# The first norm of a PEER block and its first two query tiles, done in two halves of 256 tokens, with two roundings moved

## The chip, the cores and the metric

The kernel runs on one core of one Trainium2 chip. The metric is the device time of one execution in microseconds (us). Before the change it was 3694.77 us, the median of three runs (3693.27 to 3698.32).

## The reference, cut to what matters

The program computes a two-layer transformer block (adaptive norms, gated feed-forward, token mixing) and then a second block whose last part is a PEER layer. The change touches only the step from the layer norm into that PEER layer. Here `x` has 512 tokens of 1024 channels.

```python
x = layer_norm(DEEPNORM_ALPHA * x + m, ln1_g[l], ln1_b[l])
f = peer_ffn(x, peer_wq[l], peer_keys[l], peer_u[l], peer_v[l])

def peer_ffn(x, wq, sub_keys, u_tab, v_tab):
    q = (xf @ wq).reshape(t, 8, 2, 128)                 # 8 heads, two 128-wide halves each: 16 query tiles
    scores = einsum("thpc,hpnc->thpn", q, sub_keys)     # 128 keys per half
    s_top, i_top = top_k(scores, 16)
    cand = s_top[..., 0, :, None] + s_top[..., 1, None, :]
    best_s, best_pos = top_k(cand, 16)                  # 16 of 16384 experts per token and head
    gates = softmax(best_s)
    # per token and head, over its 16 experts e:
    out += gelu(x . u_tab[e]) * gates[e] * v_tab[e]
```

## The kernel before, in words

Activations stand channels by tokens: `T.xT` is eight tiles k of 128 channels by 512 tokens. Every matrix product with a weight is made of three passes: a weight tile of 128x1024 is loaded by SP's queue into `wraw`, rounded by ACT into `whi` (`round`, line 2114), and POOL makes the remainder `wlo` (`rest`, line 2120); the activations are split in the same way into `xh` and `xl`. A tile's load waits until a buffer's earlier remainder is done (semaphore `w_lo`). The five tiles 8 to 12 (`AHEAD`) go to buffers of their own, but their loads stand in SP's queue behind the load of tile 5, which waits for the remainder of tile 3.

The last stage, `peer` (line 2131), begins when the mean and the reciprocal standard deviation of every token stand ready (`T.mean` in SBUF, `T.psN` in PSUM). The five engines then run lists of instructions that are written out by hand and joined by semaphores:

- Norm. DVE multiplies tile k by `psN` into one of two temporary tiles (line 2585), ACT applies gain and bias (2412) and rounds into `xh` (2416), DVE makes `xl` (2588). The mean is subtracted from tiles 2 to 4 by DVE (2576) and from 5 and 6 by POOL (2212). Each instruction covers all 512 tokens.
- Query tiles 0 and 1. TensorE (PE) takes the eight k in order as they come (`pair`, lines 314 to 318). ACT copies the first 128 tokens' queries (2420), PE scores them against the keys (`first_scores`, 2263), and DVE's `best` and `choose_first` find the 16 experts of the first head for the first 128 tokens.
- A gather (line 2226) is one indirect DMA issued by POOL: 128 tokens' rows of 2048 numbers (1.05 MB), u and v of one expert for each token. There are 512 of them. For the first 96 there are nine slots: five `g_own`, two `g_low` (free once query tile 3 is multiplied), two in `xT` (free once all tokens are transposed into `xtok`, `turn`, 2272). A gather into a used slot waits for the matmul that reads it (`g_mm`).
- Expert work. DVE takes the dot product with u (`dots`, 2532), ACT gelu, gate and a diagonal matrix (`weights`, 2395 to 2407), PE adds diag times v (`experts`, 2311, in the later loop 2348).
- Query tiles 2 to 4 come before the first expert work on PE; each of the tiles 5 to 15 is then cut in two parts, and four sets of two gathers stand between them (`PARTS`). After gather 96 the slots are 16 and only gathers, dots and expert matmuls are left.

POOL's list mixes gathers with the remainders; the rule is

```python
W.rest(pool, 3)
W.rest(pool, 4)
for j in range(OWN):
    gather(j)
W.rest(pool, 5)
for j in range(OWN, EARLY):
    gather(j)
W.rest(pool, 6)
for j in range(EARLY, TOTAL):
    n, at = divmod(j - EARLY + PAIR, ROWS)
    if at == 0 and STEP0 + n + 1 < NQ2 and n > 0:
        W.rest(pool, STEP0 + n + 1)
    gather(j)
```

with OWN 5, EARLY 9, PAIR 2, ROWS 8, STEP0 5, NQ2 16.

Of the kernel before, what the change touches and what calls it, by code (L numbers as in the profile page):

```python
# [15 lines left out]
F32 = mybir.dt.float32  # L16
# [2059 lines left out]


AHEAD = (8, 9, 10, 11, 12)


class Queries(Stream):
# [34 lines left out]
    def rest(self, pool, n):  # L2116
# [3 lines left out]
        self.nc.gpsimd.tensor_tensor(lo, self.raw(n), hi.bitcast(F32), ALU.subtract).then_inc(self.M["w_lo"], 1)  # L2120

    def part(self, pe, n, out, xh, xl, k0, k1):
        if k0 == 0:
            pe.wait_ge(self.M["w_lo"], n + 3)
        for k in range(k0, k1):
            mm = self.products(self.at(n), k, out, xh[:, k], xl[:, k], k == 0, k == KD - 1)
        if k1 == KD:
            mm.then_inc(self.M["w_mm"], 1)


def peer(nc, T):
# [17 lines left out]
    with ExitStack() as ctx:  # L2149
        M = T.sems.take(nc, "peer", S_SEMS + f"w_ahead*5 x_t x_n x_hi x_lo e_keys e_q e_q0 e_s0 e_s1 e_sc e_sv e_top e_ch e_x e_xo x_c x_cp g_uv*{LOW + TOPS + OWN + SPARE} "  # L2150
                                "g_dot g_gelu g_w g_diag g_mm g_ln g_wide g_lnp g_al g_ch g_st g_cp g_rt g_fin g_out g_end h_dif h_exp h_pick h_some")
# [4 lines left out]
        rest, st, mv = T.rest, T.st, T.mv  # L2156
        tmp = q
        lnp = keys[:, :, :].rearrange("p n k -> p (n k)").rearrange("p (a d) -> p a d", a=2)
# [30 lines left out]
        with nc.Block() as block:  # L2189
# [19 lines left out]
            def _(pool):  # L2209
                W.ahead(pool=pool)  # L2210
                for k in (5, 6):
                    nc.gpsimd.tensor_tensor(T.xT[:, k], T.xT[:, k], T.mean[:, :], ALU.subtract).then_inc(M["x_cp"], 1)

                def gather(j):
                    if j < TOP:
                        pool.wait_ge(M["h_some"], j // 8 + 1)
                    else:
                        pool.wait_ge(M["h_pick"], j // TOP + 1)
                    if earlier[j] is not None:
                        pool.wait_ge(M["g_mm"], earlier[j] + 1)  # L2220
                    elif slot_of[j] >= spare0:
                        pool.wait_ge(M["e_x"], 2 * TT)
                        pool.wait_ge(M["x_lo"], KD)
                    elif slot_of[j] < own0:
                        pool.wait_ge(M["w_mm"], (4 if j < FIRST else NQ2) + 4)
                    nc.gpsimd.indirect_dma_start(  # L2226
                        slots[slot_of[j]], None, T.d["uv"],
                        bass.IndirectOffsetOnAxis(ap=T.idx[:, j // TOP, j % TOP:j % TOP + 1], axis=0)
                    ).then_inc(M["g_uv"][slot_of[j]], 16)

                W.rest(pool, 3)
                W.rest(pool, 4)
                for j in range(OWN):
                    gather(j)
                W.rest(pool, 5)
                for j in range(OWN, EARLY):
                    gather(j)
                W.rest(pool, 6)
                for j in range(EARLY, TOTAL):
                    n, at = divmod(j - EARLY + PAIR, ROWS)  # L2240
                    if at == 0 and STEP0 + n + 1 < NQ2 and n > 0:
                        W.rest(pool, STEP0 + n + 1)
                    gather(j)

            @block.tensor
            def _(pe):
# [46 lines left out]
                def own_row(t):  # L2293
                    if t >= 2:
                        pe.wait_ge(M["g_cp"], t - 1)
                    pe.wait_ge(M["e_xo"], 2 * t + 2)
                    for c in range(2):
                        nc.tensor.matmul(banks[t % 2][c], aid[:, :], xtok[:, t, c * S:(c + 1) * S], start=True,
# [68 lines left out]
            def _(act):  # L2367
# [53 lines left out]
                W.round(act, 4)
                for n in range(2):
                    nc.scalar.activation(q[:, n, P:S], psQ[:, n, P:S], ACT.Copy).then_inc(M["e_q"], 1)
                turned(0)
# [59 lines left out]
            def _(dve):  # L2484
# [71 lines left out]
                def last_final():  # L2556
# [13 lines left out]
                    for h in halves:  # L2570
                        nc.vector.scalar_tensor_tensor(r[:, h], r[:, h], mv[:, 3:4], lnp[:, 1, h], ALU.mult,
                                                       ALU.add).then_inc(M["g_fin"], 1)

                for k in range(KD + 1):
                    if 1 <= k <= 3:
                        nc.vector.tensor_tensor(T.xT[:, k + 1], T.xT[:, k + 1], T.mean[:, :],
                                                ALU.subtract).then_inc(M["x_c"], 1)
                    if k < KD:
                        if k >= 2:
                            dve.wait_ge(M["x_n"], k - 1)  # L2580
                        if 2 <= k <= 4:
                            dve.wait_ge(M["x_c"], k - 1)
                        if k in (5, 6):
                            dve.wait_ge(M["x_cp"], k - 4)
                        nc.vector.tensor_tensor(tmp[:, k % 2], T.xT[:, k], T.psN[:, :], ALU.mult).then_inc(M["x_t"], 1)
                    if k:
                        dve.wait_ge(M["x_hi"], k)
                        nc.vector.tensor_tensor(xl[:, k - 1], T.xT[:, k - 1], xh[:, k - 1].bitcast(F32),
                                                ALU.subtract).then_inc(M["x_lo"], 1)
                nc.vector.tensor_scalar(aid[:, :], ident, ALPHA, None, ALU.mult).then_inc(M["g_al"], 1)  # L2590
                def half(g, which):
# [7 lines left out]
                dve.sem_inc(M["e_top"], 2)  # L2599
                choose_first(nc, T, B, link, dve, M)  # L2600
                dve.wait_ge(M["e_s1"], 2)
                best((NQ2, NQ2 + 1), [T.mean[:, n * P:(n + 1) * P] for n in range(2)])
# [300 lines left out]
```

## Time and profile before

| | us |
|---|---|
| median of the runs | 3694.77 |
| the profiled execution's own time | 3691.83 |
| its span, first to last instruction | 3690.1 |
| PE busy | 3416.0 |
| DVE busy | 2137.5 |
| POOL busy | 1686.5 |
| ACT busy | 1321.1 |
| DMA share of the gathers' queue over the span | 35.1% |

All times below are us from the span's start, in one profiled execution. Busy time is counted by engine over the whole program, so it says little of a stage; the rows further below are taken from stretches. `PEclk` is the granted TensorE clock as a share of 2.4 GHz (0.50 is 1.2 GHz). PEld is the loading of weights into TensorE. A row names the line of the kernel, the operation, what it writes and reads, its shape, and in brackets the idle time before it with the engine that ended it.

### The profile page before, as it was taken

The page shows a single profiled execution, that of the slowest core. Times are in us where ns is not written, and L with a number is a line of the kernel's source. Part 1 is how long each engine was busy: PE and PEld are TensorE (multiplying, and loading weights), DVE is VectorE, ACT ScalarE, POOL GpSimd, SP SyncE. Part 2 cuts the span into 40 slices and gives each one's busy share as a digit, 9 for nine tenths or more (in the row PEclk, how much of TensorE's full clock was granted, in tenths as well). Part 3 has the DMA queues.
Part 4 walks back from the last instruction along what each step waited for, and adds up shares of the span by engine and source line. Part 5 has one row for each costly group of instructions (what it writes and reads, how often), then busy time and mean ns, then how long its engine had stood idle before and what let it go on. Part 6 is the DMA issues. An engine that isn't in the chain of part 4 may idle for free. (4 is left out here: it accounts for less than half of the span.)

```text
span 3690.1 us, 42955 instructions
## 1 busy us (share of the span) xinstructions
PE 3416.0 (93%) x14116; PEld 2359.4 (64%) x14116; DVE 2137.5 (58%) x4134; ACT 1321.1 (36%) x2721; POOL 1686.5 (46%) x1088
## 2 busy tenths in 40 slices
PE   8999999999999999999999999999878777877887
PEld 6888876788888888876888876755433333333333
DVE  6545567433336546566333046788878768767664
ACT  3332326443323332245333233444333233223322
POOL 2545532444455445423444532455545444444542
PEclk9999999999999999999999999999989998988989
DMA  6536420133444445300233331399999999999999
GB/s 257 183 118 234 155 103 2 52 97 97 154 158 175 161 168 214 122 29 13 91 96 97 103 98 46 142 409 421 421 416 422 422 421 410 422 422 412 422 422 384
DMA packets 140782, 829.41 MB, mean 225 GB/s; under 512 B 15704, under 2 KB 16864, under 8 KB 64352
## 3 DMA queue, kind: packets, MB, share of 16 engines
q0 software_dynamic: 73728, 536.90, 35.1%
q1 hardware_dynamic: 66912, 290.73, 22.6%
q8 instruction: 75, 1.23, 0.1%
q14 instruction: 67, 0.55, 0.0%
HBM read 825.48 MB, written 2.10 MB: 224 GB/s over the span
## 5 line engine op out<-in xcount | busy, mean ns | idle before, releaser
L282 POOL TENSOR_TENSOR wlo<-wraw,whi 128x1024 fp32r<-128x1024 f32 x344 | 869.4, 2532 | 1094.7 <-ACT whi L278 1094.3
L278 ACT ACTIVATE whi<-wraw 128x1024 fp32r<-128x1024 f32 x344 | 363.5, 1058 | 642.1 <-DMA wraw<-in_wts 361.1
L289 PE MATMUL f_ps<-f_hh,whi 128*128 128x512 f32 x1344 | 522.8, 389 | 0.0
L290 PE MATMUL f_ps<-f_hl,whi 128*128 128x512 f32 x1344 | 522.8, 389 | 0.0
L291 PE MATMUL f_ps<-f_hh,wlo 128*128 128x512 f32 x1344 | 522.8, 389 | 0.0
L598 DVE TENSOR_TENSOR f_a<-f_sg,f_ps 128x512 f32<-128x512 f32 x88 | 60.5, 687 | 507.6 <-PE f_ps L291 491.6
L2226 POOL DMA_INDIRECT g_own<-in_uv,idx x185 | 217.0, 1173 | 206.1 <-PE g_psF L2348 115.0
L2395 ACT ACTIVATE g_dotb<-g_dotb 128x4 f32<-128x4 f32 (+2 forms) x164 | 33.5, 204 | 772.8 <-DVE g_dotb L2638 643.6
L2226 POOL DMA_INDIRECT g_low<-in_uv,idx x151 | 177.8, 1178 | 259.4 <-PE g_psF L2348 211.1
L2348 PE MATMUL g_psF<-g_low,g_diagb 128*128 128x512 f32 x400 | 213.9, 664 | 78.6 <-ACT g_diagb L2407 78.6
L291 PEld LDWEIGHTS f_ps<-f_hh,wlo 128*128 128x128 f32 x1344 | 252.3, 188 | 52.4
L289 PEld LDWEIGHTS f_ps<-f_hh,whi 128*128 128x128 f32 x1344 | 252.3, 188 | 52.4
L290 PEld LDWEIGHTS f_ps<-f_hl,whi 128*128 128x128 f32 x1344 | 252.3, 188 | 52.1
L2348 PE MATMUL g_psF<-g_own,g_diagb 128*128 128x512 f32 x400 | 200.3, 635 | 28.7 <-ACT g_diagb L2407 28.7
L2638 DVE CUSTOM_DVE_ANT_0 g_own<-g_own,xtok 128x1024 f32<-128x1024 f32 x125 | 151.9, 1225 | 126.3 <-DMA g_own<-in_uv,idx 125.6
L2348 PEld LDWEIGHTS g_psF<-g_low,g_diagb 128*128 128x128 f32 x400 | 84.8, 216 | 196.1 <-issue 105.4
L289 PE MATMUL f_psD<-f_ah,whi 128*128 128x512 f32 x512 | 199.2, 389 | 0.0
L290 PE MATMUL f_psD<-f_al,whi 128*128 128x512 f32 x512 | 199.2, 389 | 0.0
L291 PE MATMUL f_psD<-f_ah,wlo 128*128 128x512 f32 x512 | 199.2, 389 | 0.0
L153 DVE CUSTOM_DVE_ANT_0 m_prod<-m_wrow,crow 128x1024 f32<-128x1024 f32 x88 | 153.4, 1743 | 49.3 <-DMA m_wrow<-in_ada 40.2
L2638 DVE CUSTOM_DVE_ANT_0 g_low<-g_low,xtok 128x1024 f32<-128x1024 f32 x125 | 149.5, 1224 | 55.6 <-DMA g_low<-in_uv,idx 46.7
L657 DVE SCALAR_TENSOR_TENSOR xT<-f_psD,mod,xT 128x512 f32<-128x512 f32 (+1 forms) x36 | 24.5, 690 | 256.2 <-PE f_psD L291 256.2
(554 smaller groups left out, 7110.6 us busy)
## 6 DMA issues: line engine op xcount, KB each, us to landing
wraw<-in_wts SPq DMA_DIRECT2D x354, 512.0 KB, 3.5
m_wrow<-in_ada SPq DMA_DIRECT2D x44, 1024.0 KB, 7.5
m_erow<-in_ada SPq DMA_DIRECT2D x28, 1024.0 KB, 5.2
p_wt<-in_wtok SPq DMA_DIRECT2D x2, 3168.0 KB, 10.0
p_wt<-in_w SPq DMA_DIRECT2D x2, 3072.0 KB, 10.4
g_own<-in_uv,idx POOLq DMA_INDIRECT x185, 26.3
g_low<-in_uv,idx POOLq DMA_INDIRECT x151, 23.8
xT<-in_xT SPq DMA_DIRECT2D x2, 1024.0 KB, 17.9
```

Of the source, the lines that this page charges most:

```text
L153: nc.vector.tensor_tensor_reduce(prod, row, T.crow[:, :], 1.0, 0.0, ALU.mult, ALU.add, out).then_inc(M["m_dot"], 1)
L278: self.nc.scalar.activation(self.T.whi[:, j % 4], self.T.wraw[:, j % 2], ACT.Copy).then_inc(self.M["w_hi"], 1)
L282: self.nc.gpsimd.tensor_tensor(self.T.wlo[:, j % 4], self.T.wraw[:, j % 2], self.T.whi[:, j % 4].bitcast(F32), ALU.subtract).then_inc(self ...
L289: self.nc.tensor.matmul(out, hi, xh, start=first, stop=False)
L290: self.nc.tensor.matmul(out, hi, xl, start=False, stop=False)
L291: return self.nc.tensor.matmul(out, lo, xh, start=False, stop=last)
L598: nc.vector.tensor_tensor(a32[:, g], sg[:, g], ps[:, 2 * g + 1], ALU.mult).then_inc(M["f_prod"], 1)
L657: nc.vector.scalar_tensor_tensor(x, psD[:, o % 2, t], gate[:, o:o + 1], x, ALU.mult, ALU.add).then_inc(M["f_res"], 1)
L2226: nc.gpsimd.indirect_dma_start(slots[slot_of[j]], None, T.d["uv"], bass.IndirectOffsetOnAxis(ap=T.idx[:, j // TOP, j % TOP:j % TOP + 1], a ...
L2348: mm = nc.tensor.matmul(banks[t % 2][c], diag[:, (LOOPS + k // FOUR) % 4, k % FOUR], slots[slot_of[j]][:, D + c * S:D + (c + 1) * S], star ...
L2395: nc.scalar.activation(dot[:, s % 4, 0:size], dot[:, s % 4, 0:size], ACT.Gelu_apprx_tanh).then_inc(M["g_gelu"], 1)
L2638: nc.vector.tensor_tensor_reduce(u, u, xtok[:, t], 1.0, 0.0, ALU.mult, ALU.add, dot[:, (LOOPS + q) % 4, k:k + 1]).then_inc(M["g_dot"], 1)
```

## The change

The 512 tokens of the norm and of query tiles 0 and 1 are split in two groups of columns, `COLS` (tokens 0 to 255, then 256 to 511).

- ACT rounds weight tile 3 first of all, then does gain, bias and rounding of all eight k for group 0, then for group 1; after the second k of group 1 it copies the first 128 tokens' queries.
- DVE scales, centres and makes `xl` of group 0, then only scales and centres group 1. The scaling is done in place in `T.xT`, so the two temporary tiles and their wait are gone. POOL makes `xl` of group 1.
- PE multiplies tiles 0 and 1 for group 0 into `psX` (PSUM that the transposes use afterwards), scores the first 128 tokens, and then multiplies group 1 into `psQ` (`pair_of`: 96 matmuls of 256 columns in place of 48 of 512).
- POOL centres in four instructions of 256 columns, makes the remainder of tile 3 right after, then the eight `xl`; the remainder of tile 4 now stands behind the first five gathers, and those of tiles 7 to 15 stand four gathers later.
- The first transposes wait for all norm work and for two more copies out of `psX`; the small matrix `aid` is made after `choose_first`.

```diff
+    def pair_of(self, pe, out, xh, xl, x_hi, x_lo, done):
+        for k in range(KD):
+            w = slice(k * P, (k + 1) * P)
+            pe.wait_ge(x_hi, k + 1)
+            for j in range(2):
+                self.nc.tensor.matmul(out[:, j], self.T.whi[:, j, w], xh[:, k], start=k == 0, stop=False)
+                self.nc.tensor.matmul(out[:, j], self.T.wlo[:, j, w], xh[:, k], start=False, stop=False)
+            pe.wait_ge(x_lo, k + 1)
+            for j in range(2):
+                mm = self.nc.tensor.matmul(out[:, j], self.T.whi[:, j, w], xl[:, k], start=False, stop=k == KD - 1)
...
             def _(pool):
-                for k in (5, 6):
-                    nc.gpsimd.tensor_tensor(T.xT[:, k], T.xT[:, k], T.mean[:, :], ALU.subtract).then_inc(M["x_cp"], 1)
+                for c in COLS:
+                    for k in (5, 6):
+                        nc.gpsimd.tensor_tensor(T.xT[:, k, c], T.xT[:, k, c], T.mean[:, c],
+                                                ALU.subtract).then_inc(M["x_cp"], 1)
+                W.rest(pool, 3)
+                c = COLS[1]
+                for k in range(KD):
+                    pool.wait_ge(M["x_hi1"], k + 1)
+                    nc.gpsimd.tensor_tensor(xl[:, k, c], T.xT[:, k, c], xh[:, k, c].bitcast(F32),
+                                            ALU.subtract).then_inc(M["x_lo1"], 1)
...
-                W.rest(pool, 3)
-                W.rest(pool, 4)
                 for j in range(OWN):
                     gather(j)
+                W.rest(pool, 4)
                 W.rest(pool, 5)
...
-                    if at == 0 and STEP0 + n + 1 < NQ2 and n > 0:
+                    if at == ROWS // 2 and STEP0 + n + 1 < NQ2 and n > 0:
                         W.rest(pool, STEP0 + n + 1)
...
                 def turn(n):
-                    pe.wait_ge(M["x_n"], 4 * half + 4)
+                    pe.wait_ge(M["x_n"], 2 * KD)
...
-                W.pair(pe, psQ, xh, xl, M["x_hi"], M["x_lo"])
-                pe.wait_ge(M["g_al"], 1)
+                c = COLS[0]
+                W.pair_of(pe, psX[:, :, c], xh[:, :, c], xl[:, :, c], M["x_hi"], M["x_lo"], M["e_p0"])
                 first_scores()
+                c = COLS[1]
+                W.pair_of(pe, psQ[:, :, c], xh[:, :, c], xl[:, :, c], M["x_hi1"], M["x_lo1"], M["w_mm"])
+                pe.wait_ge(M["e_px"], 2)
...
+                def normal(a, k):
+                    c = COLS[a]
+                    act.wait_ge(M["x_t"], a * KD + k + 1)
+                    nc.scalar.activation(T.xT[:, k, c], T.xT[:, k, c], ACT.Identity, ...
+                    act.wait_ge(M["x_n"], a * KD + k + 1)
+                    nc.scalar.activation(xh[:, k, c], T.xT[:, k, c], ACT.Copy).then_inc(M["x_hi1" if a else "x_hi"], 1)
                 W.round(act, 3)
+                for k in range(KD):
+                    normal(0, k)
+                for k in range(KD):
+                    normal(1, k)
+                    if k == 1:
+                        for n in range(2):
+                            act.wait_ge(M["e_p0"], n + 1)
+                            nc.scalar.activation(q[:, n, 0:P], psX[:, n, 0:P], ACT.Copy).then_inc(M["e_q0"], 1)
+                for n in range(2):
+                    nc.scalar.activation(q[:, n, P:2 * P], psX[:, n, P:2 * P], ACT.Copy).then_inc(M["e_px"], 1)
```

Three places show the order of instructions.

POOL, from its first instruction of this stage (`wlo` is a remainder of a weight tile, `e_xl` the remainder of the activations, a DMA a gather). Before:

```order
L2212 TENSOR_TENSOR xT<-xT,mean 128x512 x2
L2120 TENSOR_TENSOR wlo<-wraw,whi 128x1024 x2
L2226 DMA g_own<-in_uv,idx 128x2048 x5
L2120 TENSOR_TENSOR wlo<-wraw,whi 128x1024
L2226 DMA g_low<-in_uv,idx 128x2048 x2
```

and now:

```order
L2227 TENSOR_TENSOR xT<-xT,mean 128x256 x4
L2121 TENSOR_TENSOR wlo<-wraw,whi 128x1024
L2233 TENSOR_TENSOR e_xl<-xT,e_xh 128x256 x8
L2249 DMA g_own<-in_uv,idx 128x2048 x5
L2121 TENSOR_TENSOR wlo<-wraw,whi 128x1024 x2
L2249 DMA g_low<-in_uv,idx 128x2048 x2
```

One remainder (tile 3) stands ahead of eight new instructions, all ahead of the first gather; the other (tile 4) moved behind five gathers.

DVE at the beginning of the same stage, now (each line before had 512 columns, and the second half of this list was part of the first):

```order
L2616 TENSOR_TENSOR xT<-xT,psN 128x256
L2620 TENSOR_TENSOR xT<-xT,mean 128x256
L2616 TENSOR_TENSOR xT<-xT,psN 128x256
L2630 TENSOR_TENSOR e_xl<-xT,e_xh 128x256
L2620 TENSOR_TENSOR xT<-xT,mean 128x256
L2616 TENSOR_TENSOR xT<-xT,psN 128x256
L2630 TENSOR_TENSOR e_xl<-xT,e_xh 128x256
L2620 TENSOR_TENSOR xT<-xT,mean 128x256
L2616 TENSOR_TENSOR xT<-xT,psN 128x256
L2630 TENSOR_TENSOR e_xl<-xT,e_xh 128x256
```

Between two scalings (2616) stands an instruction with both inputs in SBUF (2620 or 2630), and the eleven instructions of group 1 follow this list ahead of the first `best`.

ACT around the start of the copies for the first scores, now:

```order
L2439 ACTIVATE xT<-xT,q 128x256
L2443 ACTIVATE e_xh<-xT 128x256
L2453 ACTIVATE e_qb<-g_psF 128x128 x2
L2439 ACTIVATE xT<-xT,q 128x256
L2443 ACTIVATE e_xh<-xT 128x256
```

The two copies stood behind the whole norm and the rounding of tile 3; they now stand behind ten of its sixteen steps, and behind that rounding, which comes first.

## Rows read from the trace of the kernel before

**Rows 1.** Windows, end phase: busy us of each engine, clock, DMA share, GB/s
```profile
2600.00:3600.00 1000.00, 782.94 (x1670) 332.30 (x1669) 727.78 (x1821) 313.10 (x990) 483.10 (x406) 0.90 1.01 419
```

**Rows 2.** Chain that ended last, in order of time: start, us, what
```profile
2616.97 12.90 DMA g_own<-in_uv,idx
```

**Rows 3.** Timeline of DVE, norm and first choice
```profile
2361.51 1.28 DVE L2576 TENSOR_TENSOR xT<-xT,mean 128x512 f32<-128x512 f32 x1
2362.71 0.68 DVE L2585 TENSOR_TENSOR e_qb<-xT,psN 128x512 f32<-128x512 f32 x1
2363.31 1.16 DVE L2588 TENSOR_TENSOR e_xl<-xT,e_xh 128x512 fp32r<-128x512 f32 x1
...
2377.55 0.49 DVE L2490 MAX8 tops<-e_psS 128x8 f32<-128x128 f32 x2 [2.02 <-PE e_psS L2263]
```

**Rows 4.** Timeline of ACT in the norm, then one group by form
```profile
2368.90 0.80 ACT L2412 ACTIVATE xT<-e_qb,q 128x512 f32<-128x512 f32 x1
2369.73 0.63 ACT L2416 ACTIVATE e_xh<-xT 128x512 fp32r<-128x512 f32 x1
...
2374.57 1.04 ACT L2114 ACTIVATE whi<-wraw 128x1024 fp32r<-128x1024 f32 x1
...
L2381 ACT ACTIVATE e_kept<-e_psS 128x256 f32<-128x256 f32 x16 | 6.1, 383 | 25.7 <-DVEq L2507 25.7
```

**Rows 5.** Timeline of POOL from the norm to gather 15
```profile
2359.28 1.27 POOL L1810 TENSOR_TENSOR xT<-xT,mean 128x512 f32<-128x512 f32 x1 [6.18 <-ACT mean L1771]
2360.97 2.96 POOL L2212 TENSOR_TENSOR xT<-xT,mean 128x512 f32<-128x512 f32 x2 [0.41 <-POOLq L1523]
...
2384.85 1.14 POOL L2226 DMA_INDIRECT g_own<-in_uv,idx  x1 [4.42 <-DVEq L2015]
...
2393.53 0.95 POOL L2226 DMA_INDIRECT g_low<-in_uv,idx  x1 [0.16 <-PE g_psF L2272]
...
2401.29 0.94 POOL L2226 DMA_INDIRECT xT<-in_uv,idx  x1 [5.57 <-PE g_psF L2272]
...
2423.59 2.87 POOL L2120 TENSOR_TENSOR wlo<-wraw,whi 128x1024 fp32r<-128x1024 f32 x1 [2.94 <-ACT whi L2114]
2426.61 1.75 POOL L2226 DMA_INDIRECT g_low<-in_uv,idx  x1 [0.15 <-issue]
```

**Rows 6.** Timeline of DVE during the remainder of tile 7
```profile
2424.16 3.39 DVE L2532 CUSTOM_DVE_ANT_0 g_own<-g_own,xtok 128x1024 f32<-128x1024 f32 x1
```

**Rows 7.** Timeline of PE: first matmul of query tile 2, expert work, its waits
```profile
2378.14 0.47 PE L289 MATMUL e_psQ<-e_xh,whi 128*128 128x512 f32 x1
...
2405.71 1.02 PE L2311 MATMUL psN<-g_own,g_diagb 128*128 128x512 f32 x2
...
2430.02 1.10 PE L2311 MATMUL psN<-g_own,g_diagb 128*128 128x512 f32 x2 [0.59 <-ACT g_diagb L2407]
...
2440.80 1.10 PE L2311 MATMUL psN<-g_low,g_diagb 128*128 128x512 f32 x2 [0.93 <-ACT g_diagb L2407]
```

**Rows 8.** Windows from the first gathers on: last number GB/s
```profile
2380.00:2415.00 35.00, 35.00 (x169) 26.73 (x168) 30.45 (x114) 18.44 (x39) 19.40 (x16) 1.00 1.02 416
2425.00:2440.00 15.00, 14.28 (x45) 7.38 (x43) 14.47 (x40) 7.07 (x19) 9.06 (x8) 1.00 0.89 340
```

**Rows 9.** DMA issues of 2424 to 2444, then 2444 to 2480: us to landing
```profile
g_low<-in_uv,idx POOLq DMA_INDIRECT x1, 6.3
...
g_low<-in_uv,idx POOLq DMA_INDIRECT x4, 9.4
```

**Rows 10.** PEld: loads of 128 columns back to back, and one group's mean
```profile
2361.02 2.75 PEld L2320 LDWEIGHTS e_psS<-const 128*128 128x128 f32 x24 [0.61 <-issue]
...
L291 PEld LDWEIGHTS e_psQ<-e_xh,wlo 128*128 128x128 f32 x112 | 21.0, 188 | 4.5
```

**Rows 11.** Windows in which TensorE's clock fell or was low
```profile
2356.00:2358.00 2.00, 2.00 (x8) 1.33 (x8) 0.85 (x5) 0.30 (x1) 0.00 (x0) 0.62 0.00 0
2650.00:2660.00 10.00, 0.93 (x3) 0.21 (x1) 9.08 (x25) 2.54 (x8) 0.00 (x0) 0.50 1.01 421
```

More of the change, by code:

```diff
@@ L2075 @@
 SLOTS_OWN = 5
+COLS = (slice(0, S // 2), slice(S // 2, S))
 AHEAD = (8, 9, 10, 11, 12)
@@ L2120, in rest @@
         self.nc.gpsimd.tensor_tensor(lo, self.raw(n), hi.bitcast(F32), ALU.subtract).then_inc(self.M["w_lo"], 1)
+    def pair_of(self, pe, out, xh, xl, x_hi, x_lo, done):
[8 more added lines that the diff above has]
+                mm = self.nc.tensor.matmul(out[:, j], self.T.whi[:, j, w], xl[:, k], start=False, stop=k == KD - 1)
+                if k == KD - 1:
+                    mm.then_inc(done, 1)
     def part(self, pe, n, out, xh, xl, k0, k1):
@@ L2149, in peer @@
     with ExitStack() as ctx:
-        M = T.sems.take(nc, "peer", S_SEMS + f"w_ahead*5 x_t x_n x_hi x_lo e_keys e_q e_q0 e_s0 e_s1 e_sc e_sv e_top e_ch e_x e_xo x_c x_cp g_uv*{LOW + TOPS + OWN + SPARE} "
+        M = T.sems.take(nc, "peer", S_SEMS + f"w_ahead*5 x_t x_n x_hi x_hi1 x_lo x_lo1 e_p0 e_px e_keys e_q e_q0 e_s0 e_s1 e_sc e_sv e_top e_ch e_x e_xo x_c x_cp g_uv*{LOW + TOPS + OWN + SPARE} "
                                 "g_dot g_gelu g_w g_diag g_mm g_ln g_wide g_lnp g_al g_ch g_st g_cp g_rt g_fin g_out g_end h_dif h_exp h_pick h_some")
@@ L2223, in gather @@
                         pool.wait_ge(M["x_lo"], KD)
+                        pool.wait_ge(M["x_lo1"], KD)
                     elif slot_of[j] < own0:
@@ L2296, in own_row @@
                     pe.wait_ge(M["e_xo"], 2 * t + 2)
+                    pe.wait_ge(M["g_al"], 1)
                     for c in range(2):
@@ L2572, in last_final, with scaled, centred @@
                                                        ALU.add).then_inc(M["g_fin"], 1)
+                def scaled(a, k):
+                    c = COLS[a]
+                    if 2 <= k <= 4:
+                        dve.wait_ge(M["x_c"], 3 * a + k - 1)
+                    if k in (5, 6):
+                        dve.wait_ge(M["x_cp"], 2 * a + k - 4)
+                    nc.vector.tensor_tensor(T.xT[:, k, c], T.xT[:, k, c], T.psN[:, c], ALU.mult).then_inc(M["x_t"], 1)
+                def centred(a, k):
+                    c = COLS[a]
+                    nc.vector.tensor_tensor(T.xT[:, k, c], T.xT[:, k, c], T.mean[:, c], ALU.subtract).then_inc(M["x_c"], 1)
+                c = COLS[0]
                 for k in range(KD + 1):
                     if 1 <= k <= 3:
-                        nc.vector.tensor_tensor(T.xT[:, k + 1], T.xT[:, k + 1], T.mean[:, :],
-                                                ALU.subtract).then_inc(M["x_c"], 1)
+                        centred(0, k + 1)
                     if k < KD:
[L2579 to L2585, printed above, removed]
+                        scaled(0, k)
                     if k:
                         dve.wait_ge(M["x_hi"], k)
-                        nc.vector.tensor_tensor(xl[:, k - 1], T.xT[:, k - 1], xh[:, k - 1].bitcast(F32),
+                        nc.vector.tensor_tensor(xl[:, k - 1, c], T.xT[:, k - 1, c], xh[:, k - 1, c].bitcast(F32),
                                                 ALU.subtract).then_inc(M["x_lo"], 1)
-                nc.vector.tensor_scalar(aid[:, :], ident, ALPHA, None, ALU.mult).then_inc(M["g_al"], 1)
+                for k in range(KD):
+                    if 1 <= k <= 3:
+                        centred(1, k + 1)
+                    scaled(1, k)
                 def half(g, which):
@@ L2600, in _ @@
                 choose_first(nc, T, B, link, dve, M)
+                nc.vector.tensor_scalar(aid[:, :], ident, ALPHA, None, ALU.mult).then_inc(M["g_al"], 1)
                 dve.wait_ge(M["e_s1"], 2)
```

11 lines of the change are left out of this document (2 added, 9 removed).

## The prediction

> **What bounds the kernel now.** I read the windows of the end phase first. From 2600 to 3600 the DMA engines are busy throughout at 419 GB/s, while PE is busy 783 of 1000 us [rows 1]. A gather is 128 x 2048 x 4 bytes = 1.05 MB, at the 422 GB/s of the page's busiest slices 2.49 us. So the end is set by when the DMA engines start on the 512 gathers and by every us in which they then stand still; the change touches only that beginning. The chain of waits agrees: near the end of the query loop it passes over a gather's landing at 2616.97 [rows 2].
>
> The windows of the beginning come next. From 2380 to 2415 DMA moves 416 GB/s, that is without a hole; from 2425 to 2440 it moves 340, a loss of 15 x (422 - 340) / 422 = 2.9 us [rows 8]. POOL's timeline names that hole: the remainder of tile 7 waited 2.94 us for ACT, took 2.87, and gather 15 went out only at 2426.61 behind it [rows 5].
>
> Between 2378 and the end of the query loop PE is the second bound. It starts query tile 2 at 2378.14 and reads the first gathered rows at 2405.71; its only waits up to 2445 are 0.59 and 0.93 us [rows 7]. Slots come free only by its matmuls, so an earlier gather does not by itself bring the tenth one earlier.
>
> **Part 1: the norm of group 0.** ACT paces the norm: 0.80 + 0.63 = 1.43 us for each k of 512 columns [rows 4]. A copy of 256 columns takes 0.38 where 512 take 0.63 [rows 4], so I take 0.25 off both, and 1.43 - 0.50 = 0.93 for a k, 7.4 us for eight. The rounding of tile 3 (1.04 us [rows 4]) now comes first: ACT begins the norm at about 2362.0, not 2361.6. Undisturbed, group 0 would be rounded by 2369.4.
>
> But it is disturbed. A DVE instruction with both inputs in SBUF does not run beside a POOL one: the 512-column centring at 2361.51 took 1.28 us and `xl` at 2363.31 took 1.16 while POOL centred (2.96 us for its two), but the scaling at 2362.71, with an input in PSUM, took 0.68 [rows 3, 5]. The same in rows of the expert work: a dot product that began at 2424.16 took 3.39 us and ended 1.1 us after POOL's remainder did [rows 5, 6]; the page has 1225 ns as its mean. The two engines take turns instruction by instruction. The remainder of tile 3, some 2.4 us, was made behind the whole norm; now it falls inside group 0. Played through with POOL's four centrings of about 0.7 us (2.96 / 4, less the turns), POOL starts that remainder at 2364.8 and holds DVE's second `xl` until 2367.2. DVE works in order, so the fourth scaling is done at 2368.3. ACT gets that k 3.3 us late (it would have begun at 2362.0 + 3 x 0.93 = 2364.8), plus queueing, and ends group 0 at about 2372.9; before, all 512 columns were rounded at 2374.7. The last `xl` is at 2373.3.
>
> **Part 2: the way to the first gather.** DVE must still issue the eleven instructions of group 1, each about 0.34 us (half of 0.68 [rows 3]): 3.7 us, and some 0.4 of turns, so it is free at 2377.4. ACT does two more k (to 2375.5), copies two tiles of 128 columns (0.5), PE scores (0.7): the scores are ready at 2376.8. So `best` starts at 2377.4; it started at 2377.55 [rows 3]. From there to the first gather it was 2384.85 - 2377.55 = 7.3 us [rows 3, 5]; one turn lost to POOL's `xl` adds up to 0.5. First gather: 2385.2, **+0.3 us**.
>
> **Part 3: PE.** ACT does six more k of group 1 after the copies, to 2381.6; POOL's last `xl` follows by 0.7, PE's last matmuls at 2382.7, two copies out of `psX` are hidden there, two `turn`s 0.9. Query tile 2 starts at 2383.7, not 2378.14 [rows 7]: **+5.5 us**, since ACT now does one norm of two groups, 2 x 7.4 against 8 x 1.43 = 11.4, and the rest is the stall of part 1 with the copies. Everything PE does up to the first experts moves by that. The two waits of 0.59 and 0.93 then fall away, as DVE's dots there are no longer late: **+4.0** from 2445 on.
>
> **Part 4: DMA.** The loads of tiles 5 and 8 to 12 wait for tile 3's remainder, which comes at 2367.2 instead of about 2378: six loads of 0.52 MB, 7.5 us of DMA time, move from beside the first gathers to ahead of them. But the gain is spent in holes. Gathers 5 and 6 wait for query tile 3 (issued at 2393.53 before [rows 5], now about 2399), 7 and 8 for the last `turn` (2401.29 before [rows 5], now 2406.8), gather 9 for the first expert matmul (now about 2413.5). So by about 2415 the new kernel has moved nine gathers. Before, it was 35 us x 416 GB/s = 14.6 MB less eight loads (4.2 MB) = 9.9. Behind by 0.95 x 2.49 = 2.4 us.
>
> The remainder of tile 7 stands four gathers later, at a point where ACT has rounded it long before, so the hole of 2.9 us goes; I leave 0.5 for what is left. DMA alone: 2.4 - 2.9 + 0.5 = 0.0. The other bound is PE: gathers are issued 4.0 later from 2445 on. In that stretch a gather lands 9.4 us after issue, against 6.3 for one issued into an empty queue [rows 9], so 3.1 us of queue cover it, and 4.0 - 3.1 = 0.9 remain. The later one decides: **+0.9 us**. `aid` moved, 0.2 us of DVE, is hidden by the wait for the keys' scores.
>
> The profiled execution took 3691.83; it gives 3692.7. The median stands 2.9 above that execution, so I forecast **3695.7**.
>
> **Weight loads.** `pair_of` has 96 loads and matmuls in place of 48. The one matmul of 256 columns is half of the spacing of 0.23 between 512-column ones. A load's own row says 188 ns, but 24 loads stand in 2.75 us, 0.115 each [rows 10]. By 0.115 six take 0.69 us a k and hide under ACT's 0.93; by 0.188 they take 1.13, 0.2 more than ACT, 1.6 us for a group, PE 3 us later. I take the back-to-back row. The Trainium skill, TensorE: Matmul & The Clock Gate, section LDWEIGHTS (loading the stationary operand), gives columns / 1.2 ns, an estimate of 107 ns for 128 columns: by it six take 0.64 and the sum stays as it is.
>
> **One-input instructions.** No row shows a DVE instruction with one SBUF input waiting for POOL. If those of `choose_first` do, the first gather is later by up to 1.5 us, which PE's 5.5 mostly hides: +0.5 at the end, inside the range. The Trainium skill, SBUF — State Buffer, section SBUF: two separate sides, counts such instructions in a 2-port mode among those that exclude GpSimd; the estimate from it is that same +0.5.
>
> **Rivals.**
> 1. The remainder of tile 3 hardly stops DVE, because the turns fall otherwise. For: only one instruction is in its way. Against: it takes 2.4 us beside a group of 7.4. Then group 0 ends at 2369.4, the first gather goes at 2381.5 and query tile 2 starts 2 us late. DMA is 1.2 ahead at 2415 with 2.4 of the hole gained: 3.6 us faster, 3691. Chance 0.21.
> 2. PE does not bind: moved loads, earlier gathers and the closed hole all count, 7.5 + 2.9 less a hole or two of 2 us, 8 us faster, 3686. It needs slots to come free earlier, which no row promises. Chance 0.04.
> 3. TensorE's clock falls. It was at 0.62 in a stretch with eight matmuls in 2 us of one-column and narrow ones, and at 0.50 when PE had stood still [rows 11]. In the new norm PE waits up to 4 us for tile 3's remainder and later has 0.69 us of work for each 0.93. At 1.2 GHz a k takes 1.38 us on PE: eight k of group 1 are 3.6 us later, and query tile 2, 5.5 us at full clock, loses up to 3 more. With the half in group 0 PE is 5 to 8 us later still, and as the queue's 3.1 us are used up, all of it reaches the end: 3700 to 3704, slower than before. It decides once the clock is low for more than about 3 us of that stretch. Chance 0.15, half of it above 3702.
>
> **How the numbers follow.** What a measurement can tell here is 0.2%, 7.4 us. The forecast has 0.60. Rivals 1 and 3 lie within 7.4 us for the most part. Faster by more: 0.05 (rival 2 and the tail of 1). Slower by more: 0.09 (rival 3's upper half and an unforeseen wait). No change: 0.86. The range reaches from rival 1, less 2 for the scatter of the runs, to the middle of rival 3: 3689 to 3702.
>
> **What would show it.** Right: the second `xl` of group 0 takes about 2 us beside tile 3's remainder; first gather within 1 us of 2385; first matmul of tile 2 at 2382 to 2385; six loads landed before the first gather; 300 to 400 GB/s with holes between 2395 and 2415; no hole at 2425. Wrong: a first gather before 2382, PE's tile 2 within 1 us of 2378, or a clock below 1.00 between 2365 and 2395.

## The result, and the profile after

The changed kernel takes **3703.39 us** (median of 9 runs) beside 3696.75 for the kernel before. The medians differ by 6.6 us; the ratio of the two is estimated at 1.0023, 95% interval 1.0015 to 1.0032, so 5.5 to 11.8 us slower. The forecast was 3695.7, its range ended at 3702.

The profiled execution of the changed kernel is 13.1 us late before this stage begins: GpSimd's first centring stands at 2374.07, at 2360.97 before [rows 5]. That is scatter of the layers ahead, which both kernels share: in the other runs below, with the same layers, it stands between 2360.58 and 2373.24. So I count from that instruction, and call what lies between it and the end of the span the **stage**: 3690.1 - 2360.97 = 1329.1 us before, 3710.7 - 2374.07 = 1336.6 after, **+7.5**. "At 14.1" is 14.1 us after that instruction. One execution of each kernel was profiled, so how much the stage scatters was not measured. Two runs below in which the transfers are as far as before have stages 0.3 and 1.1 us shorter, so I read no cause into differences of about 1 us.

The page of the changed kernel, its first part and the chain that ended last:

```profile
PE 3427.3 (92%) x14164; PEld 2372.6 (64%) x14164; DVE 2148.4 (58%) x4145; ACT 1324.1 (36%) x2739; POOL 1701.0 (46%) x1098
...
DMA 16%; PE 9%; DVE 6%; issue 3%; ACT 1%; POOL 1%; DVEq 0%; SPq 0%; POOLq 0%
```

Busy time (PE +11.3, DVE +10.9 over before) doesn't say where the 7.5 us arise. Its ScalarE timeline does (start, duration, line, operation, idle time before it and who ended it):

```profile
2377.21 1.06 ACT L2115 ACTIVATE whi<-wraw 128x1024 fp32r<-128x1024 f32 x1 [4.90 <-SPq L257]
2378.17 0.58 ACT L2439 ACTIVATE xT<-xT,q 128x256 f32<-128x256 f32 x1
...
2381.69 0.60 ACT L2439 ACTIVATE xT<-xT,q 128x256 f32<-128x256 f32 x1 [1.54 <-DVE xT L2616]
```

The rounding of tile 3 now stands in front, and it waits for SyncE's queue: L257 raises the count of the weight loads that are there already, and SyncE comes to it only after it has cleared the last stage's 56 semaphores. The norm begins at 4.10, where I had it at 1.03 (2362.0). The idle 1.54 is the forecast stall: VectorE was held by tile 3's remainder. VectorE and GpSimd of the same kernel:

```profile
2379.24 1.75 DVE L2630 TENSOR_TENSOR e_xl<-xT,e_xh 128x256 fp32r<-128x256 f32 x1 [3.83 <-ACT e_xh L2443]
```

```profile
2374.07 2.96 POOL L2227 TENSOR_TENSOR xT<-xT,mean 128x256 f32<-128x256 f32 x4 [0.41 <-POOLq L1523]
2378.34 2.36 POOL L2121 TENSOR_TENSOR wlo<-wraw,whi 128x1024 fp32r<-128x1024 f32 x1 [1.32 <-ACT whi L2115]
```

TensorE: the first scores, query tile 2 (2378.14 before [rows 7]), and two waits in the loop; then GpSimd's eighth gather.

```profile
2390.79 0.68 PE L2285 MATMUL e_psS<-e_keysb,e_qb 128*128 128x128 f32 x4 [1.75 <-ACT e_qb L2453]
...
2398.30 0.47 PE L289 MATMUL e_psQ<-e_xh,whi 128*128 128x512 f32 x1
...
2460.99 1.10 PE L2334 MATMUL psN<-g_low,g_diagb 128*128 128x512 f32 x2 [1.80 <-ACT g_diagb L2433]
2502.82 1.10 PE L2334 MATMUL psN<-g_own,g_diagb 128*128 128x512 f32 x2 [1.36 <-ACT g_diagb L2433]
```

```profile
2421.44 0.94 POOL L2249 DMA_INDIRECT xT<-in_uv,idx  x1 [6.77 <-PE g_psF L2294]
```

Query tile 2 starts at 24.23; before it was 17.17: **+7.06**, forecast +5.5. The waits, forecast to vanish (0.59 and 0.93 before [rows 7]), are there, and larger. The eighth gather, released by TensorE, is issued at 47.37; before it was 40.32 [rows 5], so it is 7.05 later. Of stretches (busy us of each engine with counts, granted clock, DMA share, GB/s):

```profile
2374.00:2380.00 6.00, 3.66 (x28) 3.29 (x28) 2.16 (x4) 2.72 (x5) 4.61 (x5) 0.98 0.29 83
2380.00:2386.00 6.00, 5.01 (x24) 4.96 (x24) 5.27 (x14) 4.33 (x10) 0.70 (x1) 0.50 0.92 359
2386.00:2392.00 6.00, 4.25 (x33) 4.08 (x33) 5.30 (x15) 5.02 (x13) 1.79 (x3) 0.95 0.92 346
...
2420.00:2430.00 10.00, 10.00 (x41) 6.33 (x40) 9.70 (x26) 6.53 (x16) 6.32 (x4) 1.00 0.83 310
```

TensorE's clock fell to 0.50, the lower of its levels [rows 11], for some 6 us after it had stood 2.19 us for the first rounded activations, which are late because of tile 3. The DMA engines had holes past 2420: that gather had waited 6.77 us for TensorE, and the next but one (gather 9 of part 4) stood behind the remainder of tile 6.

### The profile page after: what moved, and what is told of

Same layout as the page of the kernel before. It is cut to its first block and busy times, and to the rows that moved or that the text cites. A ratio compares the mean times of both kernels' runs of the same rounds, so it can differ in the third digit from the quotient of the medians.

```text
span 3710.7 us, 43089 instructions
## 1 busy us (share of the span) xinstructions
PE 3427.3 (92%) x14164; PEld 2372.6 (64%) x14164; DVE 2148.4 (58%) x4145; ACT 1324.1 (36%) x2739; POOL 1701.0 (46%) x1098
```

## The experiments

One table first. "Late" is what the DMA engines had moved less than before by 150 us of the stage, as time at 419 GB/s, added up from windows (good to about 0.2). From then on they are nearly full in every run, so what is late there mostly stays so. "Rests" are the remainders of the weight tiles from the loop on.

| run | tile 2 starts at | late | stage | ratio to before, 95% |
|---|---|---|---|---|
| before | 17.17 | 0 | 1329.1 | |
| changed kernel | 24.23 | 7.7 | 1336.6 | 1.0023 (1.0015 to 1.0032) |
| rests later alone | 17.17 | 1.4 | 1329.6 | 1.0004 (0.9995 to 1.0013) |
| split alone | 24.23 | 7.4 | 1335.9 | 1.0018 (1.0009 to 1.0026) |
| count raised first | 23.33 | 7.4 | 1336.1 | 1.0011 (1.0002 to 1.0019) |
| tile 3 behind | 21.04 | 6.7 | 1336.1 | 1.0012 (1.0004 to 1.0021) |
| tile 3 behind, rests old | 21.04 | 4.0 | 1332.8 | 1.0008 (0.9999 to 1.0017) |
| the same, clock kept | 20.61 | 5.0 | 1333.1 | 1.0009 (1.0000 to 1.0018) |
| before, TensorE late | 32.37 | 15.1 | 1344.2 | 1.0039 (1.0024 to 1.0055) |
| before, gathers late | 17.18 | 0.5 | 1328.6 | 0.9993 (0.9983 to 1.0002) |
| before, rest 7 later | 17.18 | 0.0 | 1328.0 | 0.9994 (0.9985 to 1.0003) |
| before, TensorE early | 17.19 | -1.2 | 1326.7 | 1.0001 (0.9990 to 1.0012) |
| before, loads ahead | 17.17 | 0.0 | 1328.8 | 1.0003 (0.9993 to 1.0013) |
| before, both | 17.18 | -1.6 | 1326.8 | 1.0003 (0.9993 to 1.0012) |

### The two halves of the change

```diff
-                    if at == 0 and STEP0 + n + 1 < NQ2 and n > 0:
+                    if at == ROWS // 2 and STEP0 + n + 1 < NQ2 and n > 0:
```

> The kernel before with one number changed: from the loop on, GpSimd forms a weight tile's remainder four gathers later; norm and first query tiles as before. Theory A (the loss is PE's: query tile 2 starts 7 us later than before, and that reaches the end): nothing here is late, so 3695 to 3698 us against 3696.7, ratio 0.9995 to 1.0005. Theory B (the loss is the loop's: the later remainder holds VectorE, two SBUF inputs each, just while it chooses the best candidates, and PE loses 1.4 to 1.8 us on every second query tile): most of the +8.5 us is here already, 3701 to 3705 us, ratio 1.0012 to 1.0023, and the trace shows PE waits of over 1 us beside the candidates' sums.

The split alone is the changed kernel with that line as before.

> The changed kernel with the remainders of the loop at their old place (first of eight gathers): only the split of norm, rounding and first query tiles is left. Theory A: 3703 to 3706 us, ratio 1.0018 to 1.0026, as the changed kernel. Theory B: 3696 to 3699 us, ratio 1.0000 to 1.0006. If each part has its share, both this and the run with the remainders alone lie between.

The split carries the loss: +6.8 us of stage against +0.5 for the later rests, and of the two only the split's ratio has an interval above 1. But the rests are not free. With them later the DMA engines are 2.9 us ahead at 80, since the hole around tile 7 is gone, and 1.4 behind at 150. Every second query tile VectorE is held at its choice. The changed kernel's rows, VectorE and GpSimd:

```profile
2452.05 2.59 DVE L2038 TENSOR_TENSOR h_candb<-tops 128x256 f32<-128x256 f32 x1
```

```profile
2451.82 2.54 POOL L2121 TENSOR_TENSOR wlo<-wraw,whi 128x1024 fp32r<-128x1024 f32 x1
```

The same `TENSOR_TENSOR` of 128x256 took 0.44 in the first choice, at 2395.06. VectorE's dot products stand behind the choice, and TensorE waits for them by way of ScalarE's diagonal matrix, in the run with the rests alone too:

```profile
2449.76 1.10 PE L2311 MATMUL psN<-g_low,g_diagb 128*128 128x512 f32 x2 [1.77 <-ACT g_diagb L2407]
2491.58 1.10 PE L2311 MATMUL psN<-g_own,g_diagb 128*128 128x512 f32 x2 [1.36 <-ACT g_diagb L2407]
```

Is the first of them worth keeping alone?

```diff
-                    if at == 0 and STEP0 + n + 1 < NQ2 and n > 0:
+                    if at == (ROWS // 2 if n == 1 else 0) and STEP0 + n + 1 < NQ2 and n > 0:
```

> The kernel before, but the remainder of weight tile 7 alone is formed four gathers later; the others stay at their places. In the run with all of them later the gathers were 2.9 us ahead of before after 80 us of the stage (the hole around tile 7 is gone) and 1.4 us behind after 150 us. If the loss comes from the remainders of tiles 8 and 9 only, the 2.9 us are kept: stage 1326 to 1327 us, time 3693 to 3695, ratio 0.9990 to 0.9996. If the moved remainder itself brings the loss with it, stage 1329 to 1330 and no difference.

2.8 us ahead at 80 us, 0.0 at 150: the lead is not kept, though no later rest was moved. TensorE loses 1.77 in one wait where it lost 0.59 and 0.93, and a gather can't be issued before TensorE has freed its buffer. The stage is 1.1 shorter, the ratio's interval holds 1.

### Is it TensorE's lateness?

```diff
+                    if n == 2:
+                        for _ in range(68):
+                            nc.tensor.matmul(psQ[:, 0, 0:P], ident, ident, start=True, stop=True)
                     W.part(pe, n, psQ[:, n % 2], xh, xl, k0, k1)
```

> The kernel before, with 68 matmuls of 128 columns on the identity put ahead of query tile 2's matmuls (about 7 us of TensorE, whose results are overwritten), nothing else: TensorE is then as late as in the changed kernel, the first gathers are not. The stage's own time, from GpSimd's first centring to the end of the span, is 1329.1 us before and 1336.6 in the changed kernel. Theory A (TensorE's lateness at query tile 2 goes through to the end in full, since TensorE frees the buffers that the gathers wait for): stage 1335 to 1337 us, time +6 to +8 us. Theory C (what counts is the start of the gathers and the order in the DMA queue): stage 1329 to 1332.

The dose was twice what I meant: the 68 matmuls are 136 instructions in the trace, 0.11 us each. TensorE's timeline:

```profile
2385.50 15.35 PE L2281 MATMUL e_psQ<-const 128*128 128x128 f32 x136
2400.61 0.48 PE L289 MATMUL e_psQ<-e_xh,whi 128*128 128x512 f32 x1
```

Query tile 2 was 15.2 us late, and the stage is 15.0 longer. All of it goes through, in a kernel in which nothing else was changed. TensorE is fully busy meanwhile, and the DMA engines starve, at 41, 51 and 61 us of the stage:

```profile
2409.00:2419.00 10.00, 10.00 (x54) 8.56 (x53) 6.88 (x36) 4.41 (x8) 1.89 (x2) 1.00 0.37 125
2419.00:2429.00 10.00, 10.00 (x52) 7.74 (x51) 8.15 (x27) 6.86 (x16) 3.16 (x3) 1.00 0.67 252
2429.00:2439.00 10.00, 10.00 (x30) 5.48 (x29) 9.72 (x24) 5.61 (x14) 6.66 (x5) 1.00 0.75 288
```

At the same place the kernel before moved:

```profile
2401.00:2411.00 10.00, 10.00 (x35) 5.78 (x35) 8.86 (x24) 6.78 (x19) 7.16 (x5) 1.00 1.01 422
2411.00:2421.00 10.00, 10.00 (x31) 5.41 (x30) 9.37 (x35) 4.21 (x9) 4.50 (x5) 1.00 1.01 420
```

The rival to this is the start of the gathers.

```diff
                 W.rest(pool, 4)
+                pool.wait_ge(M["h_some"], 1)
+                nc.gpsimd.tensor_tensor(T.own[:, 4, 0:D].rearrange("p (a b) -> p a b", b=P), ident.unsqueeze(1).to_broadcast([P, 8, P]), ident.unsqueeze(1).to_broadcast([P, 8, P]), ALU.subtract).then_inc(M["x_cp"], 1)
+                pool.wait_ge(M["x_cp"], 3)
```

> The kernel before, with one idle subtraction of 128x1024 (about 2.4 us) on GpSimd between the choice of the first eight experts and the first gather: all five first gathers start some 2.4 us later, TensorE's query tiles do not. Theory A: stage under 1330 us, time within 1 us of before. Theory C: stage 1331 to 1332 us, +2 us or more.

The first gather went at 25.9 instead of 23.9, and the eighth, which waits for TensorE, at 40.3 in both. The stage is not longer, so a start of the gathers later by 2.0 costs nothing; in the changed kernel it was 1.7 (25.62 against 23.88). Theory C falls. Its other half, the order of the loads in the queue, is tested further below (loads ahead: 1328.8, no gain).

### What made query tile 2 late?

```diff
-                T.sems.zero_before(sp)
                 W.ahead(sp=sp)
+                T.sems.zero_before(sp)
```

> The changed kernel, but SyncE raises the count of the weight loads that are there already before it clears the last stage's 56 semaphores, not after: ScalarE's rounding of tile 3 need not wait 3.1 us. Theory A: the norm starts some 3.1 us earlier, query tile 2 starts 2 to 3.1 us earlier (part of it may be lost again to VectorE and GpSimd holding each other), and the run is as much shorter: 3700 to 3702 us, ratio 1.0010 to 1.0016. Theory B: under 1 us, 3702.5 to 3704.5, ratio about 1.002.

ScalarE's and VectorE's rows, and two windows of this run:

```profile
2366.27 1.06 ACT L2115 ACTIVATE whi<-wraw 128x1024 fp32r<-128x1024 f32 x1 [1.90 <-PEq L263]
2367.24 0.58 ACT L2439 ACTIVATE xT<-xT,q 128x256 f32<-128x256 f32 x1
...
2369.97 0.60 ACT L2439 ACTIVATE xT<-xT,q 128x256 f32<-128x256 f32 x1 [0.76 <-DVE xT L2616]
...
2372.81 0.60 ACT L2439 ACTIVATE xT<-xT,q 128x256 f32<-128x256 f32 x1 [1.79 <-DVE xT L2616]
```

```profile
2369.86 2.25 DVE L2630 TENSOR_TENSOR e_xl<-xT,e_xh 128x256 fp32r<-128x256 f32 x1
```

```profile
2382.00:2384.00 2.00, 2.00 (x12) 2.00 (x11) 1.93 (x12) 1.94 (x5) 1.60 (x3) 0.53 0.33 122
2384.00:2386.00 2.00, 2.00 (x13) 2.00 (x12) 1.78 (x9) 1.91 (x6) 1.58 (x3) 0.62 0.01 3
```

The norm starts at 1.10, 3.0 us earlier. In group 0 ScalarE now waits for VectorE twice, 0.76 and 1.79 instead of 1.54 once: a centring is held by GpSimd's centring, and then tile 3's remainder holds the second `xl` for 2.25, not the first for 1.75. So ScalarE ends the norm only 2.0 earlier. Then the low clock falls into group 1, where TensorE has no slack: from the end of ScalarE's norm to query tile 2 it is 3.1 us, 2.0 in the changed kernel. Query tile 2 gains 0.9. My expectation of 2 to 3.1 missed it: a wait removed at the head was partly paid again at the next ones.

Then both of tile 3's steps out of the way:

```diff
-                W.round(act, 3)
                 for k in range(KD):
                     normal(0, k)
...
+                W.round(act, 3)
                 for n in range(2):
                     nc.scalar.activation(q[:, n, P:2 * P], psX[:, n, P:2 * P], ACT.Copy).then_inc(M["e_px"], 1)
...
-                W.rest(pool, 3)
                 c = COLS[1]
...
+                W.rest(pool, 3)
                 for j in range(OWN):
                     gather(j)
...
-                for n in (4, 5) + AHEAD + (6, 7) + tuple(range(AHEAD[-1] + 1, NQ2)):
+                for n in (4,) + AHEAD + (5,) + (6, 7) + tuple(range(AHEAD[-1] + 1, NQ2)):
```

> The changed kernel with weight tile 3 taken out of the way: ScalarE rounds it behind the last column of the second group, GpSimd forms its remainder behind the eight remainders of the second group, and SyncE issues the five loads ahead of the load that needs tile 3's old buffer. The wait of 3.1 us and the 1.5 us that VectorE stood still for GpSimd in group 0 both go. Theory A: query tile 2 starts 4 to 5 us earlier than in the changed kernel: 3698.5 to 3700 us, ratio 1.0005 to 1.0010. Theory B: within 1.5 us of the changed kernel, 3702 to 3705. If the order of the DMAs around the first gathers counts instead (theory C: weight loads stand in the queue ahead of the first gathers), the loads that now start 3 us earlier give back up to 2 us more.

> The changed kernel with tile 3 taken out of the norm's way (rounded behind the second group) and the loop's remainders at their old places. Query tile 2 starts 3.9 us later than before instead of 7.05. Theory A: stage 1329.1 + 3.9 = 1333.0 us (1332.5 to 1333.5, if TensorE's clock holds; the earlier run of this norm lost another 1.7 us to a granted clock of 0.72 for 5 us), time +3 to +5 us. If the split costs 7 us by something that the start of query tile 2 does not show: 1336 again.

In both, the norm starts at 0.4, ScalarE ends it at 18.0, and query tile 2 starts at 21.04, 3.9 late. With the rests at their old places the stage is 3.7 longer: again all of it. With the rests later it is 7.0 longer. A wait of 1.95 at 84 us of the stage was followed by a lower clock:

```profile
2448.00:2450.00 2.00, 1.15 (x2) 0.63 (x3) 2.00 (x5) 1.97 (x6) 1.47 (x1) 0.77 0.97 381
2450.00:2452.00 2.00, 2.00 (x3) 0.66 (x2) 2.00 (x3) 1.70 (x6) 0.00 (x0) 0.50 0.98 377
2452.00:2454.00 2.00, 2.00 (x6) 0.90 (x4) 1.90 (x9) 1.38 (x5) 0.83 (x1) 0.88 1.02 430
```

From TensorE's part before this to its next wait (84.2 to 127.7, 43.5 us) the run with the rests alone took 41.8: 1.7 us more. After the waits of 1.77 in the run with the rests alone and 1.80 in the changed kernel the clock held at 1.00. One execution shows the fall, so its chance stays open. With 3.9, 0.5 and 1.7 accounted for, 0.9 of the 7.0 stays unexplained.

Of the 3.9 that are left, TensorE's low clock in group 1 was one suspect. ScalarE, GpSimd's last `xl` and three windows of the run with tile 3 behind, rests old:

```profile
2378.12 0.42 ACT L2443 ACTIVATE e_xh<-xT 128x256 fp32r<-128x256 f32 x1
```

```profile
2378.61 0.74 POOL L2232 TENSOR_TENSOR e_xl<-xT,e_xh 128x256 fp32r<-128x256 f32 x1 [0.18 <-ACT e_xh L2443]
```

```profile
2371.00:2373.00 2.00, 0.00 (x0) 0.00 (x0) 2.00 (x6) 1.94 (x7) 1.09 (x2) 1.00 1.03 381
2373.00:2375.00 2.00, 1.96 (x11) 1.99 (x12) 1.97 (x9) 1.94 (x5) 1.26 (x3) 0.61 1.06 401
2375.00:2377.00 2.00, 2.00 (x12) 2.00 (x12) 1.93 (x13) 1.94 (x5) 1.58 (x3) 0.54 0.48 175
```

```diff
+                for n in range(4):
+                    for t in range(TT):
+                        nc.tensor.matmul(psS[:, 1, t * P:(t + 1) * P], ident, ident, start=True, stop=True)
                 first_scores()
```

> The run with tile 3 behind the norm and the remainders at their old places, and 16 idle matmuls of 128 columns (1.9 us) in the 2.3 us that TensorE stands still between group 0's products and the first scores. In that run the granted clock then fell to 0.50 for 3 us, group 1's first products took 1.28 us a column block in place of 0.71, and TensorE ended group 1 1.5 us behind GpSimd's last remainder. Theory A with the clock as the remaining part: no fall, query tile 2 starts 1.1 us earlier (19.9 us after the stage's start), stage 1331.7 us in place of 1332.8, time +2 to +3 over before. If the clock is not what holds group 1 there: query tile 2 stays at 21.0, stage 1332.8. In neither case is it below the kernel before, since ScalarE alone needs until 18.0 us of the stage for two groups, against 14 for the whole width.

```profile
2376.95 3.74 PE L2348 MATMUL e_psS<-const 128*128 128x128 f32 x32
2380.52 0.61 PE L2285 MATMUL e_psS<-e_keysb,e_qb 128*128 128x128 f32 x4
...
2387.51 0.47 PE L289 MATMUL e_psQ<-e_xh,whi 128*128 128x512 f32 x1
```

```profile
2379.00:2381.00 2.00, 2.00 (x21) 2.00 (x20) 1.69 (x6) 1.94 (x6) 1.43 (x2) 1.00 1.05 396
2381.00:2383.00 2.00, 2.00 (x20) 2.00 (x18) 1.76 (x11) 1.94 (x6) 1.48 (x2) 1.00 0.61 225
```

The clock stays at 1.00. My filler was again twice too long (3.74 us, not 1.9), so the first scores start at 13.62 instead of 12.46. Yet query tile 2 starts 0.4 earlier: group 1 took 6.2 us instead of 7.8 from the scores to the first `turn`. The clock was worth 1.6, the filler gave 1.2 back, and the time can't be told from the run without it. The stage isn't shorter either (1333.1); at 69.4 TensorE loses 0.94 in a wait that the run without the filler doesn't have. A filler of the right length wasn't tried. GpSimd's last `xl` ends at 18.8, and two matmuls and the transposes, some 1.0 us, must follow, so my estimate is that it makes at most 1.2 of the 3.9 good. The larger part stays with ScalarE: it has rounded the last activations at 18.0, where the whole width was done at 13.7 before.

### Could an earlier TensorE have gained?

```diff
-        for k in range(k0, k1):
+        for k in (0, 7) if n == 2 else range(k0, k1):
             mm = self.products(self.at(n), k, out, xh[:, k], xl[:, k], k == 0, k == KD - 1)
```

> The kernel before, with six of the eight column blocks of query tile 2's product left out (18 of its 24 matmuls, 4.1 us of TensorE; so the scores of query tile 2 are not those of the reference): TensorE is 4.1 us early from query tile 3 on. If the stage follows TensorE in this direction too, as it did over 3.9, 7.0 and 15.2 us of lateness: stage 1325.0 us, time -4. If the kernel before was balanced, so that the DMA engines, full from 20 to 65 us of the stage, hold from here on: stage 1327.5 to 1329, time 0 to -1.5, and the gain of an earlier query tile 2 could never have been had by the split alone.

> The kernel before, but SyncE issues the five loads of weight tiles 8 to 12 ahead of tile 5's, which waits for tile 3's remainder: they run between 5 and 15 us of the stage, where the DMA engines stand idle, and are gone before the first gather. If the DMA queue ahead of the gathers costs anything in the kernel before: stage 1324 to 1327 us, time -2 to -5. If TensorE sets the pace alone: stage 1328.5 to 1329.5, no difference.

> Both edits together: TensorE 4.1 us early at query tile 3 (18 matmuls of query tile 2 left out) and the five loads ahead. If each alone is held by the other resource, this is the only one of the three that is shorter by 3 to 4 us: stage 1325 to 1326 us. If TensorE's time goes through in both directions, it is as the run with TensorE early alone.

Two of these runs leave out 18 of the 24 matmuls of query tile 2, so they compute wrong scores for it and serve only as a measurement. TensorE started query tile 3 only 3.0 early, since the scores now wait for VectorE, and lost 2 of that again by 79, most of it at 63.7 us, where it waits for dot products that stand behind VectorE's choice:

```profile
2385.09 1.58 PE L2255 MATMUL e_psS<-e_keysb,e_qb 128*128 128x128 f32 x12 [0.85 <-DVEq L2599]
...
2429.11 1.10 PE L2311 MATMUL psN<-xT,g_diagb 128*128 128x512 f32 x2 [1.64 <-ACT g_diagb L2407]
```

After 150 us 1.2 us are left of it, 1.6 with the loads ahead. The loads alone bring nothing. In time none of the three differs from before. So lateness goes through whole; of the earliness about two fifths are left in the transfers. The stage is 2.4 shorter, which is more, but with differences of 1 us unread and the ratio's interval from 0.9990 to 1.0012 neither share is settled. What the waits do show is that VectorE stands close behind TensorE in the first 80 us.

## Why the prediction was wrong

**Failed first: part 1, the start of the norm.** "2362.0" left out that a rounding of tile 3 in front waits for a count that SyncE raises behind 56 clears. It could have been seen in advance: the wait stands in the code, and in the kernel before the rounding came at 13.6 us of the stage, long after the count. It put the norm 3.1 later, of which 1.5 reached query tile 2 (+7.06 instead of +5.5). The rest went under the stall of group 0, which I had counted too long: ScalarE lost 1.54 to it, not the 3.5 between 2369.4 and 2372.9.

**Failed most: part 4, the queue as a cover.** I let TensorE's lateness be covered by 3.1 us of queue, the difference of two landing times [rows 9]. Doses of 3.9, 7.06 and 15.2 us give stages 3.7, 6.8 and 15.0 longer. The last one is a delay of TensorE and nothing else; the other two are the split itself, with the rests at their old places. Two runs lie 0.5 to 0.8 above this line: with the clock kept 3.4 gave 4.0, and with the count raised first and the later rests 6.2 gave 7.0. Nothing was covered. A landing time says how long a gather stands in the queue; but the queue is fed by the very buffers that TensorE frees, so when TensorE is late it drains.

**Failed too: part 3, the two waits that fall away** (-1.5). With the rests at their old places they are there unchanged, 0.61 and 0.93. The whole loop has moved by 7 us: these waits stand at 76.1 and 86.9 there, at 69.1 and 79.8 before. So VectorE's dots moved with it.

**The later rests.** The closed hole was right (2.9 us ahead at 80), but that gain could not be kept, and the remainders now hold VectorE at its choice. I had forecast -2.9 + 0.5; the run alone gives +0.5 for the stage, no more than what I leave unread, and 1.4 late in the transfers.

The sum: +0.9 forecast; 1.5 for the start and 1.5 and 3.1 for the waits and the cover give 7.0, against 6.8 for the split; with the later rests it is 7.5.

**Right:** that VectorE and GpSimd hold each other there (on the first `xl`, not the second); the weight loads, hidden at 0.118 a matmul of 256 columns; 0.94 for each k on ScalarE; the weight loads done before the first gather (the DMA engines stand still from 2392); the holes of the transfers that follow. **Missed:** the first gather came at 25.6, forecast 24.2, 0.4 beyond the margin that I gave; query tile 2 starts at 24.23, where my margin ended at 24.0; and one of my signs of being wrong came true, a clock below 1.00 in the norm.

**Rival 3** gives the right time (3700 to 3704) by the wrong way. The clock did fall, but in group 0, where TensorE had slack: it ended group 0 1.75 us before the scores could start, which waited for ScalarE's copies, and the clock was back at 1.00 in group 1. Where it fell into group 1 it cost 1.1 (count raised first) and 1.6 (tile 3 behind, rests old). Rival 1 (2 us late) is refuted by 7.06, rival 2 (8 us faster) by the result and by the run with the loads ahead.

**One-input instructions** were a left-open price. Some do wait. VectorE and GpSimd of the changed kernel:

```profile
2395.43 0.17 DVE L2011 CAST h_tib<-tops 128x32 f32<-128x32 uint32 x1
...
2396.62 0.52 DVE L1987 TENSOR_SCALAR h_partb<-h_posb 128x8 uint32<-128x8 uint32 x1
2397.05 0.16 DVE L1988 TENSOR_SCALAR h_partb<-h_posb 128x8 uint32<-128x8 uint32 x1
```

```profile
2395.43 0.77 POOL L2233 TENSOR_TENSOR e_xl<-xT,e_xh 128x256 fp32r<-128x256 f32 x1 [0.21 <-ACT e_xh L2443]
2396.37 0.74 POOL L2233 TENSOR_TENSOR e_xl<-xT,e_xh 128x256 fp32r<-128x256 f32 x1 [0.17 <-ACT e_xh L2443]
```

The Trainium skill, SBUF — State Buffer, section SBUF: two separate sides, says that such instructions in a 2-port mode exclude GpSimd; the row at 2396.62 agrees, with 0.52 us where the same line took 0.17 in the kernel before; in which mode it ran the trace doesn't tell. The cast at 2395.43 took 0.17 beside GpSimd's subtraction and was not held. In the run with the clock kept, where the scores came so late that tile 3's remainder met the choice, the same line was held much longer:

```profile
2386.14 2.18 DVE L1987 TENSOR_SCALAR h_partb<-h_posb 128x8 uint32<-128x8 uint32 x1
```

```profile
2385.89 2.39 POOL L2121 TENSOR_TENSOR wlo<-wraw,whi 128x1024 fp32r<-128x1024 f32 x1 [0.18 <-ACT whi L2115]
```

## What to carry to other kernels

Where gathers wait for buffers that TensorE frees, TensorE's lateness can be the transfers' lateness: here 3.9, 7.06 and 15.2 us went through whole, though gathers landed 3.1 us later in the full queue than in an empty one. Test that by adding idle matmuls before you plan to be late, and read the length of the filler from the trace: mine was twice what I meant, two times. When an instruction is moved to the head of a stage, list every semaphore that it waits for, and ask where the engine that raises each of them stands at that moment, its housekeeping included. Count from the first instruction of the stage that you changed: in a program that scattered by 13 us ahead of it, differences of a few us could be read so, and an account of the bytes moved by a given moment told 1.4 us from 0.0.

## Not expected of the hardware

SyncE's next count, behind 56 semaphore clears, came 3.1 us after the stage's start; with the count ahead of the clears ScalarE's norm began 3.0 us earlier. Short idle of TensorE, 2.3 us in front of the first scores, was followed by some 3 us at 0.50, and 1.95 us in the loop by some 2; after waits of 1.77 and 1.80 in the loop it stayed at 1.00; one filler kept the clock at 1.00. While GpSimd took 2.54 us for a remainder, a two-input instruction of VectorE of a shape that took 0.44 elsewhere took 2.59, and a one-input instruction of 128x8 numbers took 2.18 where it took 0.17 in the kernel before.
